# The forgetting heads' half of the output product, moved into the stick-breaking heads

## The reference

```
def rmsnorm(x, g):
    y = xf * lax.rsqrt(jnp.mean(xf * xf, axis=-1, keepdims=True) + EPS)
    return (y * g.astype(jnp.float32)).astype(x.dtype)

def sb_attend(q, k, v, q_pos, k_pos):
    z = einsum("bqhd,bkhd->bhqk", q, k) * (HEAD_DIM ** -0.5)
    log_1m = jnp.where(mask, jax.nn.log_sigmoid(-z), 0.0)
    suffix = lax.cumsum(log_1m, axis=3, reverse=True) - log_1m
    a = jnp.where(mask, jnp.exp(jax.nn.log_sigmoid(z) + suffix), 0.0)
    return einsum("bhqk,bkhd->bqhd", a, v)

def merge(oa, za, ob, zb, gn_a, gn_b, w_out):
    ya = rmsnorm(oa.reshape(b, t, WIDTH_A), gn_a) * jax.nn.silu(za)
    yb = rmsnorm(ob.reshape(b, t, WIDTH_B), gn_b) * jax.nn.silu(zb)
    return einsum("bte,ed->btd", jnp.concatenate([ya, yb], axis=-1), w_out)

xp = xp + merge(oa, za, ob, zb, out_norm_a[l], out_norm_b[l], w_out[l])
y_prompt = rmsnorm(xp, final_norm_g)
```

## Time and profile before

| | us |
|---|---|
| runs | 1220.12, 1236.76, 1225.51 (median 1225.51) |
| profiled execution, time | 1224.03 |
| profiled execution, span | 1222.2 |
| TensorE busy | 1086.2 (89%) |
| VectorE busy | 721.5 (59%) |
| ScalarE busy | 438.9 (36%) |
| GpSimd busy | 221.0 (18%) |
| mean granted TensorE clock | 0.964 |

### The profile page before, as it was taken

The page is one execution under the profiler, slowest core; times in us unless marked ns, Lnnn a source line. Parts: engine busy times, 40 slices in busy tenths (PEclk is TensorE's granted clock), DMA queues, the critical chain, the costliest instruction groups (busy, mean ns, idle before and its releaser), DMA issues.

```text
span 1222.2 us, 28388 instructions
## 1 busy us (share of the span) xinstructions
PE 1086.2 (89%) x11873; PEld 915.8 (75%) x11873; DVE 721.5 (59%) x1016; ACT 438.9 (36%) x819; POOL 221.0 (18%) x152
## 2 busy tenths in 40 slices
PE   5899999899899999689969999989878888869997
PEld 5888998788788788678848787767656666657885
DVE  4423555155355457477556616676779999964653
ACT  4412222112212222022222226666665655633421
POOL 3100000000000000011111008000023464435550
PEclk9999999899999999899989999999999999978999
DMA  7391667698797987888988767424422422211332
GB/s 198 99 241 38 178 208 225 244 337 225 310 332 294 321 280 253 223 306 307 247 318 287 251 209 231 99 71 91 87 44 44 78 50 46 95 35 53 108 133 86
DMA packets 152032, 222.50 MB, mean 182 GB/s; under 512 B 92264, under 2 KB 128104, under 8 KB 135536
## 3 DMA queue, kind: packets, MB, share of 16 engines
q1 hardware_dynamic: 131184, 201.98, 53.6%
q10 hardware_dynamic: 20736, 18.88, 4.5%
HBM read 197.17 MB, written 23.66 MB: 181 GB/s over the span
## 4 chain that ended last, share of the span: by engine, by line
PE 65%; DVE 12%; DMA 9%; issue 8%; ACT 3%; POOL 1%; SPq 1%; ACTq 0%; DVEq 0%; POOLq 0%
PE bank L727 23%; PE bank L1537 7%; PE bank L800 6%; PE bank L1068 5%; PE bank L1024 5%; PE bank L1044 4%; DMA v_ring<-in_cache_fox_v 4%; PE bank L840 3%; PE bank L1005 3%; DVE k_buf L623 2%; DMA x_in<-in_x_prompt 2%; PE bank L827 2%; DVE om L1233 2%; DVE q_cur L616 2%; DMA k_buf<-in_cache_sb_k 2%
## 5 line engine op out<-in xcount | busy, mean ns | idle before, releaser
L727 PE MATMUL bank<-w_hi,hT_hi 128*128 128x256 f32 x1152 | 339.3, 294 | 2.7 <-ACT u_out L443 1.8
L727 PE MATMUL bank<-w_lo,hT_hi 128*128 128x256 f32 x1152 | 329.8, 286 | 0.0
L727 PE MATMUL bank<-w_hi,hT_lo 128*128 128x256 f32 x1152 | 329.2, 286 | 0.0
L727 PEld LDWEIGHTS bank<-w_hi,hT_hi 128*128 128x128 f32 x1152 | 225.0, 195 | 12.3 <-issue 8.1
L727 PEld LDWEIGHTS bank<-w_lo,hT_hi 128*128 128x128 f32 x1152 | 225.2, 196 | 0.0
L727 PEld LDWEIGHTS bank<-w_hi,hT_lo 128*128 128x128 f32 x1152 | 224.9, 195 | 0.0
L443 ACT ACTIVATE u_out<-bank 128x256 f32<-128x256 f32 x144 | 55.1, 383 | 428.7 <-PE bank L727 427.7
L623 DVE STREAM_TRANSPOSE k_buf<-k_buf 128x2048 f32<-128x2048 f32 x64 | 144.4, 2287 | 31.7 <-DMA k_buf<-in_cache_fox_k 19.6
L1291 POOL TENSOR_TENSOR pr<-pr,om 128x1023 f32<-128x1023 f32 (+3 forms) x64 | 93.4, 1466 | 227.7 <-DVE om L1233 224.5
L1068 PE MATMUL bank<-pT,v_nat 128*64 128x128 f32 x1152 | 99.7, 287 | 6.8 <-issue 4.5
L1233 DVE TENSOR_TENSOR_SCAN om<-om 128x1024 f32<-128x1024 f32 (+3 forms) x64 | 100.2, 1565 | 3.5 <-ACT om L1156 2.8
(11 more groups left out here) (169 smaller groups left out, 1672.6 us busy)
## 6 DMA issues: line engine op xcount, KB each, us to landing
k_buf<-in_cache_fox_k SPq DMA_DIRECT2D x32, 1024.0 KB, 10.3
v_ring<-in_cache_fox_v SPq DMA_DIRECT2D x32, 1024.0 KB, 9.3
k_buf<-in_cache_sb_k SPq DMA_DIRECT2D x32, 1024.0 KB, 8.5
v_ring<-in_cache_sb_v SPq DMA_DIRECT2D x32, 1024.0 KB, 7.8
w_raw<-in_w_in SPq DMA_DIRECT2D x15, 1024.0 KB, 14.3
out<-u_out ACTq DMA_DIRECT2D x72, 128.0 KB, 6.0
k_nat<-out SPq DMA_DIRECT2D x32, 256.0 KB, 4.0
q_nat<-q_scratch SPq DMA_DIRECT2D x32, 256.0 KB, 4.9
```

The source lines that it names most:

```text
L727: mm = pe.matmul(bank[:, U + i % 2, 0:NCOL], a[:, k, hcols(s)], b[c % 2][:, k, :], start=(k == 0 and n == 0), stop=(k == KD - 1 and n == 2))
```

## The change

The kernel takes the A half of the output product for the eight prompt tiles into the eight stick-breaking heads, one tile a head. For that:

- `out_norm_a` and `out_norm_b` are loaded as columns and multiplied into w_out by GpSimd, ahead of its split.
- o_nat is filled in another order of tiles (slot), so that tiles 4 to 7 come first.
- In head h, slot s = h - 8: ScalarE `a_gate` (sigmoid of z, at u = 6 of the head before), GpSimd `a_silu` and `a_gain` (z * sigmoid, * o_nat), TensorE `a_turn` (4 transposes, at the end of u = 1), ScalarE `a_high`, VectorE `a_low` (end of u = 2), TensorE `a_product` in two parts of 12 matmuls, ahead of the transposes of u = 3 and u = 4, ScalarE `a_move` with the row's factor as scale, beside them `a_square`, `a_mean`, `a_root` for that factor.
- The merge has ten rounds r of half the size: r = 0 and 1 are the two halves of the sample tile, whose turns are done in the last head; r = 2 to 9 are the B halves of the prompt tiles. x is added on GpSimd (`add_x`), factor and sum are one VectorE instruction (`b_out`).
- The working tiles are placed elsewhere; the loads of z and x are cut to fit.

The diff, cut to its core:

```diff
@@ pe_prompt
+                if g and u < 2 and later(head_of(p, hh), NHEAD // 2 + 1):
+                    pe.wait_ge(pa_moved, 2 * (head_of(p, hh) - NHEAD // 2) - 1 + u)
...
                     if ahead:
                         scores(*ahead, g_ahead)
+                    if g and u in PRODUCT_AT:
+                        a_product(pe, h, PRODUCT_AT.index(u))
                     transpose_p(p, hh, u, g)
...
+                    if g and u == TURN_A_AT:
+                        a_turn(pe, h)
+                    if u == TURN_A_AT + 1 and isinstance(p, int) and p == NPAIR:
+                        s_turn(pe, h, hh)
+                    if u in (5, 6) and following is None:
+                        b_turn(pe, u - 5)
...
             outputs(2 * NPAIR - 1, 1, NU - 1, 1)
+            b_product(pe, 0)
@@ act_prompt
+                    if g and u == TURN_A_AT + 1:
+                        a_high(act, h)
+                    if g and u - 1 in PRODUCT_AT:
+                        a_move(act, h, PRODUCT_AT.index(u - 1))
...
+                    if g and u == 0:
+                        a_square(act, h)
+                    if u == GATE_A_AT and following and (g or (hh and g_next)):
+                        a_gate(act, h + 1)
+                    if u in (0, 2) and following is None:
+                        b_gate(act, u // 2)
@@ dve_prompt
                     if u in PREP_AT and following:
                         prep(*following, PREP_AT[u])
+                    if g and u == TURN_A_AT:
+                        a_mean(dve, h)
+                    if g and u == TURN_A_AT + 1:
+                        a_low(dve, h)
+                    if u in (6, 7) and following is None:
+                        b_low(dve, u - 6)
@@ pool_prompt
                     pool.tensor_tensor(x, x, om[:, u % 4, 1:n], ALU.mult).then_inc(pb_ready, 1)
+                    if u == 0:
+                        a_silu(pool, h)
+                    if u == 1:
+                        a_gain(pool, h)
+                    if u == 4:
+                        a_root(pool, h)
+                    if h == NHEAD - 1 and u in (2, 4):
+                        b_silu(pool, u // 2 - 1)
+                    if h == NHEAD - 1 and u in (3, 5):
+                        b_gain(pool, u // 2 - 1)
@@ new, with TURN_A_AT, PRODUCT_AT, GATE_A_AT = 1, (3, 4), 6
+                gain = gn_col[:, 2 * c:2 * c + 2].unsqueeze(2).to_broadcast([P, 2, D])
+                pool.tensor_tensor(raw, raw, gain, ALU.mult).then_inc(wog_done, 1)
...
+        def a_silu(pool, h):
+            pool.wait_ge(sga_done, slot_of(h) + 1)
+            pool.tensor_tensor(za[:], za[:], sa[:], ALU.mult).then_inc(zga_done, 1)
...
+        def a_gain(pool, h):
+            s = slot_of(h)
+            pool.wait_ge(on_done, halves_done(s))
+            pool.wait_ge(zga_done, s + 1)
+            pool.tensor_tensor(za[:], za[:], o_nat[:, s, 0:W], ALU.mult).then_inc(yga_done, 1)
...
+        def a_turn(pe, h):
+            pe.wait_ge(yga_done, slot_of(h) + 1)
+            pe.wait_ge(s_moved, NU * h + 3)
+            for j in range(NPAIR):
+                mm = pe.transpose(bank[:, SC + 1, j * P:j * P + P], za[:, j * P:j * P + P], ident[:])
+            mm.then_inc(yta_ready, 1)
...
+        def a_low(dve, h):
+            dve.wait_ge(yahi_done, slot_of(h) + 1)
+            dve.tensor_tensor(yaT_lo[:], in_four(bank[:, SC + 1, :]), yaT_hi[:].bitcast(F32), ALU.subtract
+                              ).then_inc(yalo_done, 1)
...
+        def three_products(pe, out, hi, lo, first, cols):
+            for k in range(NPAIR):
+                for n, (a, b) in enumerate(((hi, wo_hi), (hi, wo_lo), (lo, wo_hi))):
+                    mm = pe.matmul(out, a[:, k, :], b[:, first + k, cols], start=(k == 0 and n == 0),
+                                   stop=(k == NPAIR - 1 and n == 2))
+            return mm
+
+        def a_product(pe, h, part):
+            s = slot_of(h)
+            if part == 0:
+                pe.wait_ge(yalo_done, s + 1)
+                pe.wait_ge(wolo_done, 2)
+            else:
+                pe.wait_ge(s_moved, NU * h + 4)
...
+            three_products(pe, bank[:, SC + 1 + 2 * part, :], yaT_hi, yaT_lo, 0, slice(part * W, part * W + W)
+                           ).then_inc(pa_ready, 1)
...
+        def a_move(act, h, part):
+            s = slot_of(h)
+            act.wait_ge(pa_ready, 2 * s + part + 1)
+            act.wait_ge(ra_done, s + 1)
+            act.activation(row(y_right if part else o_nat[:, :, 0:W], s), bank[:, SC + 1 + 2 * part, :], ACT.Copy,
+                           scale=row(m_stat[:, 2, :, 0:1], s)).then_inc(pa_moved, 1)
...
+        def b_product(pe, r):
+            pe.wait_ge(ylb_done, r + 1)
...
+            for part in range(2):
+                if r >= 2:
+                    pe.wait_ge(xo_done, 2 * (r - 2) + part + 1)
+                three_products(pe, bank[:, 2 * (r % 2) + part, :], yT_hi[:, r % 2], yT_lo[:, r % 2], NPAIR * int(r > 0),
+                               slice(part * W, part * W + W)).then_inc(yp_ready, 1)
...
+        def add_x(pool, r):
+            i = r - 1
+            pool.wait_ge(xm_loaded[i % 3], 16 * (i // 3 + 1))
+            pool.wait_ge(pa_moved, 2 * i)
+            for part in range(2):
+                acc = so_far(r, part)
+                pool.tensor_tensor(acc, acc, xt[:, i % 3, part * W:part * W + W], ALU.add).then_inc(xa_done, 1)
...
         def act_merge(act):
+            for r in range(1, NR + 1):
+                if r + 1 < NR:
+                    b_high(act, r + 1)
+                if r + 3 < NR:
+                    b_gate(act, r + 3)
+                if r + 1 < NR:
+                    b_square(act, r + 1)
+                if r >= 2:
+                    f_square(act, r - 1)
...
         def dve_merge(dve):
+            b_out(dve, 0, 0)
+            b_out(dve, 0, 1)
+            for r in range(1, NR + 1):
+                if r >= 2:
+                    b_out(dve, r - 1, 1)
+                if r + 1 < NR:
+                    b_low(dve, r + 1)
+                if r >= 2:
+                    f_mean(dve, r - 1)
+                if r + 1 < NR:
+                    b_mean(dve, r + 1)
+                if r + 2 < NR:
+                    b_gain(dve, r + 2)
+                if r >= 2:
+                    finish(dve, r - 1)
+                if r < NR:
+                    b_out(dve, r, 0)
 
         def pool_merge(pool):
+            b_silu(pool, 2)
+            b_root(pool, 0)
+            b_root(pool, 1)
+            b_silu(pool, 3)
+            for r in range(1, NR + 1):
+                if r + 1 < NR:
+                    b_root(pool, r + 1)
+                    add_x(pool, r + 1)
+                if r >= 2:
+                    f_root(pool, r - 1)
+                if r + 3 < NR:
+                    b_silu(pool, r + 3)
```

More of the change, by code:

```diff
@@ L974, in sp_prompt @@
                 next_pair(p, 0)
-            next_pair(NPAIR - 1, 1)
-            next_pair(NPAIR, 1)
-            with sp.Fori(NPAIR + 1, 2 * NPAIR - 1) as p:
+            for p in range(NPAIR - 1, 2 * NPAIR - 1):
                 next_pair(p, 1)
+            load_a(sp, TP - 1)
         def prep_bank(h, m):
@@ L1283, in pool_prompt @@
             split_wo(pool)
-            with pool.Fori(8, NHEAD) as h:
+            for h in range(NHEAD // 2, NHEAD):
                 for u in range(NU):
@@ new lines, in tile_rows, with slot_of, halves_done, load_gn @@
+        def tile_rows(s):
+            t = (s + TP // 2) % TP
+            return slice(t * P, t * P + P)
+        def slot_of(h):
+            return h - NHEAD // 2
+        def halves_done(s):
+            return NHEAD - 1 if isinstance(s, int) and s == 0 else NHEAD
+        def load_gn(sp):
+            with nc.allow_non_contiguous_dma(reason="1024 values in all"):
+                for g, source in enumerate((out_norm_a, out_norm_b)):
+                    sp.dma_start(gn_col[:, NPAIR * g:NPAIR * g + NPAIR], source.rearrange("o (k p) -> p (o k)", p=P)
+                                 ).then_inc(gn_loaded, 16)
@@ new lines, in f_square, with f_mean @@
+        def f_square(act, r):
+            for part in range(2):
+                act.wait_ge(xo_done, 2 * r + part + 1)
+                act.wait_ge(sqb_done, min(r + 3, NR))
+                if r > 1 or part:
+                    act.wait_ge(xsq_done, 2 * (r - 1) + part)
+                act.activation(junk[:], o_nat[:, slot_in(r), part * W:part * W + W], ACT.Square,
+                               accum_out=m_stat[:, 0, slot_in(r), 2 + part:3 + part]).then_inc(xsq_done, 1)
+        def f_mean(dve, r):
+            s = slot_in(r)
+            first, both = m_stat[:, 1, s, 2:3], m_stat[:, 1, s, 3:4]
+            dve.wait_ge(xsq_done, 2 * r - 1)
+            dve.tensor_scalar(first, m_stat[:, 0, s, 2:3], 1.0 / D, EPS, ALU.mult, ALU.add).then_inc(xms_done, 1)
+            dve.wait_ge(xsq_done, 2 * r)
+            dve.wait_ge(xms_done, 2 * r - 1)
```

(13 more changed lines are left out.)

432 lines of the change are left out of this document (237 added, 195 removed).

## The result

The changed kernel takes 1264.71 us (median, 1260.21 to 1271.88) against 1226.32 us for the kernel before on the same chip: ratio 1.031, 95% interval 1.022 to 1.040. It is slower. The forecast was 1246, the range 1210 to 1275; "slower", which it is, had been given 0.36, less than the 0.51 of "within 2%". The profiled execution took 1260.21 us, its span is 1258.6, 36.4 more than the 1222.2 of before.

A forecast was written before the change was run, and what follows sets the result against it. The prediction took heads to be held by VectorE and the merge by TensorE. Span 1222.2 + 73.1 (heads) - 51.0 (merge) = 1244.3, a forecast time of 1246 us, range 1210 to 1275.

The forecast's parts named there:

- the forecast's own case: Whole kernel: longer heads less the time the merge gives back, 1246 us, range 1232 to 1260; chance 0.55.
- Part 0: First 12 product matmuls, ahead of u=3's transposes: VectorE idle from a_low until transposes land, 2.8 + 0.7 = 3.5 us.
- the rival of the clock: Heads: TensorE's clock at its lower level behind the wait, 4.7 us more a head, 1260 to 1284 us; chance 0.17.
- Part 1: Second 12 product matmuls, ahead of u=4's transposes: copies(3) to copy(4) grows from 2.07 to 4.8 us, adding 2.7.
- the 0.2 to unit 5: In a head, a further delay up to unit 5, behind the product's second 12 matmuls: 0.2 us.
- VectorE's own: In a head, a_low (0.67) and a_mean (0.1) on VectorE count in full: 0.8 us.
- a_silu and a_gain: GpSimd in a head: a_silu ahead of the 768-wide scan costs VectorE 1.0 us, a_gain delaying later products 0.65.
- The merge: After the heads: rounds of 8.6 us, 83.1 us in all instead of 134.1, giving back 51.0.
- The products hide: Heads: TensorE has room for the product, so a head adds only 2.45 us, 1194 us in all; chance 0.13.
- The rival between: One part of the heads' product hides, or the merge runs at TensorE's pace: 1219 to 1231 us; chance 0.15.

The follow-up runs named there:

- few products: The changed kernel with each part of the product in a head cut from 12 matmuls to one, all waits and moves kept: 1219.17 us, ratio 0.992.
- the best kernel: The changed kernel with the product in four pieces at the ends of units 1 to 4, GpSimd work reordered, f_root ahead of add_x: 1220.26 us, ratio 0.994.

## Why the prediction was right and where it was off

The sign, the mechanism and the shape held, and the time lies in the range, though above the forecast's own case and not in the class that was thought likeliest. The size of a head's loss was short by 2.1 us (11.0 against 8.9), and the span by 14 us: heads 83.4 against 73.1, the merge's gain 48.4 against 51.0, and 1.5 us ahead of head 8. All three errors go the same way; none hid another.

*Part 0, the mis-sized term.* Forecast 3.5, measured 5.22: 4.45 for twelve matmuls and 0.72 from transpose to copy. The 0.7 was right, the 2.8 was not. "Waits of 1 us in every head leave the clock at 1.00" was the argument against the rival of the clock; here the wait is 2.27 us, and behind it the clock is down. Two runs settle that it is the clock: with the wait filled, and with the clock up because of the order on GpSimd, the stall is 3.67. The rival's price was too high, 4.7 a head for both parts: only part 0 is slow, by 4.45 - 2.8 = 1.65, and part 1 runs at 2.84. Its place was right, in the middle heads, and its time, 1260 to 1284, holds the 1264.7, at a third of its price in more heads. The forecast's own case (1232 to 1260) missed it. The rival had been given 0.17 and deserved more. The clock is low a second time in the head, at u=1 (0.54), which the forecast did not have either; it is part of the late k split below.

*Part 1.* Forecast 2.7: from copies(3) to copy(4) it takes 1028.76 to 1033.80, 5.04, against 2.07 before, 2.97 more. Held. So did the 0.2 to unit 5: 2.71 against 2.32, 0.39.

*VectorE's own.* a_low and a_mean 0.83, as forecast (0.8).

*a_silu and a_gain.* a_silu was put at 1.0 on the 768-wide scan, measured 0.84 (2.58 against 1.74). a_gain's 0.65 did not appear where it was put (512-wide scan 1.70, before 1.75); instead VectorE waits 1.02 for the k split, which the forecast did not have. The 1.65 of the forecast for both against 0.84 + 1.02 = 1.86 is thus near by luck in its second half. Of the 1.02 some 0.4, by estimate, are the low clock at u=1: with the same order on GpSimd, but u=1's value products at full pace, the wait is 0.55 (product behind the transposes) and 0.65 (few products). Moving both away from there, with the product of u=1 made to wait, did give the 1.86 back although the wait for a_low stood as before (2.32): the head fell from 34.05 to 30.75, the other 1.55 being part 0's clock. So the terms do come on top of the wait. Without products the same move gave nothing (27.25 against 27.07), because there the clock fell behind the wait (with a_gain's 0.35 beside the 256-wide scan).

From the 1024-wide scan to copies(3) the head takes 25.70 us against 18.04, 7.66 more: 5.22 + 0.83 + 0.84 + 1.02 = 7.91, less some 0.25 of single instructions. With 2.97 and 0.39 that is 11.02.

*The merge.* Forecast 8.6 a round and 83.1 in all, measured 8.91 and 85.66. The sum had finish behind b_silu, 1.2 + 1.3; the 2.30 of finish beside b_silu is the same thing. b_root takes 0.93 in a round, not 0.6, which is about the difference. With f_root first the round is 6.43, near TensorE's 6.05.

*The products hide.* This rival fell: even in the best order the head is 28.64, 5.6 longer than before, which is what 24 matmuls cost in the merge. A head had 3.9 us in which TensorE was idle; in the best kernel, with 24 matmuls and four transposes more, 3.8 are left (28.64 - 24.83). Next to none of the idle time was filled. The rival between, one part hidden or the merge at TensorE's pace, fell too: VectorE waits for both parts (5.22 and 2.30), and the round is 8.91.

*Where the best kernel's time comes from.* From the last 1024-wide scan to the end it takes 1210.6 - 1111.05 = 99.6 us, before 1222.2 - 1062.96 = 159.2: 59.7 less. From head 8's scan to that one it takes 211.7 instead of 166.7, 45.1 more, of which heads 8 and 9 make 7.8 and 9.6. It begins head 8 3.0 later. 59.7 - 45.1 - 3.0 = 11.6, the difference of the spans; the medians differ by 8.2.

## What to carry to other kernels

An engine with idle time in a stage takes more work for nothing only if the work stands where the engine is idle and if nothing that the bound engine waits for is queued behind it; find the instruction behind the insertion, and who waits for it. A moved product that waits for a value from the bound engine costs something even when the product is made almost nothing: with one matmul in place of twelve the head stays 4.0 us longer, by the rows some 1.9 of it behind the wait and the rest in the work beside it. An instruction moved to an engine's idle time holds up what is queued behind it as soon as its own input is late, as a_gain does in head 9. Where a new wait of some 2 us is put before matmuls, work the sum out at both clocks, and look for the cheap edits beside the main one: the order of two calls in the merge was worth 13.6 us by the medians.

## What the runs showed of the hardware

*A race for SBUF by hundredths.* The same pair of a 768-wide scan and an 895-wide GpSimd product ran in one order when the scan started 0.06 us ahead (scan 1.74 us) and in the other when it started 0.03 us behind (scan 3.36). A wait that fixes the order made a head 3.75 us shorter, clock included. The Trainium skill (SBUF — State Buffer, "Who interferes with whom") says that whoever issues first gets the shared ports for the whole instruction; the trace agrees, and adds how small the lead may be.

*The clock.* The length of a wait did not decide what the clock did behind it. TensorE waits 2.27 us for a_low in the changed kernel and the granted clock is 0.62 behind it; with GpSimd's product held back it waits 2.32 us at the same place and the clock stays at 1.00; with few products it waits 2.27 and the clock stays at 1.00 too, though it had been low at u=1 (0.53 from 1002.40 to 1006.00); with few products and GpSimd's product held back it waits 2.32 and the clock is 0.56 from a microsecond behind the wait. In the last two kernels the low stretch only changed its place. Filling the wait with matmuls kept the pace at 0.23 us. What decides in between these runs is not shown. The Trainium skill (TensorE: Matmul & The Clock Gate, "What's actually happening") has the half clock as the default that activity lifts, which the filled wait bears out.
